# Seven products for a 2x2 block matrix product: another set, four of which are added up in PSUM

## The chip, the cores and the metric

One NeuronCore of a Trainium2 chip runs the whole program. The metric is the device time of one execution in microseconds (us). One execution was also recorded by the profiler; its span runs from the first to the last instruction. In the rows, PE is TensorE (PEld its weight loads), DVE is VectorE, ACT is ScalarE, POOL is GpSimd and SP is the engine that issues most transfers.

## The reference

Two layers over 512 tokens of width 1024. The part that changes is the second half of each layer's MLP:

```python
h = rms_norm(x, norm_ffn[l])
x = x + jnp.square(jax.nn.relu(h @ w_up[l])) @ w_down[l]      # w_up 1024x4096, w_down 4096x1024, float32
```

## The kernel before, in words

All matrix products run on float32 data that is split in two: a rounded high part (`whi`, `xhi`, `fhi`; written by ScalarE) and the rest (`wlo`, `xlo`, `flo`; written by VectorE, in some stages by GpSimd), and each product is three matmuls of 128x128 by 512 (low weights times high data, high by high, high weights by low data).

The MLP's 4096 hidden columns are worked in four quarters (`QUARTERS`) for each layer, eight in the program. A quarter has two phases:

- **Up.** Eight blocks of hidden columns (`up`, 24 matmuls of 512 columns each). ScalarE takes each block's relu and square into `hid` (`hidden`). After each pair j of blocks VectorE makes the factors from the 2x2 blocks A11, A12, A21, A22 (two halves of the tokens by two halves of the pair's columns), ScalarE writes their high parts (`factors_high`), VectorE their low ones (`factors_low`). A11's own parts are made ahead of the others (`a11_high`, `a11_low`).
- **Down.** The 2x2 block product with `w_down` is made from seven products instead of eight (a Strassen form). Product r takes one factor and one weight (a block of `w_down` or a sum of blocks), 24 matmuls: four pairs j, two token tiles k, three matmuls each, into two PSUM banks (k = 0 and 1). `PRODUCTS` names for each the factor, the pair of banks, and the blocks of `xt` (the residual) to which VectorE adds it (`add_product`): 12 blocks per quarter for each k, with 24 VectorE instructions.

Each product's weight is two rows of 128x1024 (g = 0, 1). They come by transfers into eight `raw` slots (four of them named `rawx`). Four of the products need sums of two blocks, made by transfers that GpSimd issues with an adding write (`add_block`); one sum is made by VectorE (`sum_m1`). ScalarE's copy to `whi` runs five rows (`SLOTS`) ahead of TensorE: it waits for `w_used`, which TensorE raises when a row's last matmul is done. `low` is the VectorE instruction behind it.

The order on each engine is written out by hand: TensorE's M3, M4, M2, M1, M6, M5, M7; VectorE's in the list at the end of the quarter's loop. A product that takes over a bank waits until VectorE has read the one before (`READ_BEFORE`: M1 after M3, M6 after M4, M5 after M2, M7 after M1), each time with two other products between. In a layer's last quarter the last two products run tile by tile (`last_products`), and the next norm, or in the second layer the final norm and the stores of the output, follows behind.

Of the kernel before, what the change touches and what calls it, by code (L numbers as in the profile page):

```python
# [37 lines left out]
A12, A11, A22, F1, F7, F2, F5, F6, A21 = range(9)  # L38
# [29 lines left out]
QUARTER_LOADS = (4, 4, 4, 4, 1, 1, 1, 1)  # L68
QUARTER_ADDS = 2
# [33 lines left out]
def block_loads(l, q, r, g):  # L103

    slot = PRODUCT_SLOT[r] + g
    late = 4 if r in (M6, M7) else 3 if r in (M3, M4) else 1
    return loads(l, slot) + MIX_LOADS[slot] + q * QUARTER_LOADS[slot] + late


def block_adds(l, q, r):  # L110

    return (l * QUARTERS + q) * QUARTER_ADDS + (2 if r in (M6, M7) else 1)
# [34 lines left out]
def summed_weights(l, q, g):  # L147

    return (l * QUARTERS + q) * 2 + g + 1
# [7 lines left out]
def adds_of(r):  # L157
    return len(PRODUCTS[r][2])


ADDS_DOWN = 2 * sum(adds_of(r) for r in range(len(PRODUCTS)))
# [9 lines left out]
def added_down(l, q, r, k):  # L171

    i = 2 * sum(adds_of(p) for p in range(r)) + (k + 1) * adds_of(r)
    if q == QUARTERS - 1 and r == M5:
        i += k * adds_of(M7)
    elif q == QUARTERS - 1 and r == M7:
        i -= (1 - k) * adds_of(M5)
    return l * ADDS + 2 * NT + q * ADDS_DOWN + i
# [20 lines left out]
def build(nc, x, gains, weights, sinks, ws, bs, alibi, ident_in, out):  # L199
    with ExitStack() as ctx:  # L200
# [31 lines left out]
        sb("rest", [P, 896])  # L232
# [90 lines left out]
        hid_ready = sem("hid_ready")  # L323
        factors_ready = sem("factors_ready")
# [41 lines left out]
        def _(sp):  # L366
# [3 lines left out]
            def load_mix(l, pos):  # L370
                if pos >= 4:
                    wait_low(sp, nth(l, pos - 4))
                elif l:
                    wait_low(sp, nth(l - 1, down_pos(QUARTERS - 1, M7 if pos < 2 else M6, pos % 2)))
                load(l * LAYER_ROWS + pos, mix_slot(pos))

            def load_up(l, q, i):
                if i >= 4:
                    wait_low(sp, nth(l, up_pos(q, i - 4)))
                elif q == 0:  # L380
                    wait_low(sp, nth(l, MLP_POS - 4 + i))
                else:
                    wait_low(sp, nth(l, down_pos(q - 1, M6 if i < 2 else M7, i % 2)))
                load(l * LAYER_ROWS + MLP_POS + q * QUARTER_ROWS + i, i % 4)

            def load_block(l, q, r, g):

                if r in (M3, M4):
                    wait_low(sp, nth(l, up_pos(q, 4 + PRODUCT_SLOT[r] + g)))
                elif r in (M6, M7):  # L390
                    wait_low(sp, nth(l, down_pos(q, M3 if r == M6 else M4, g)))
                elif q == 0:
                    sp.wait_ge(w_used, nth(l, wo_pos(1, 3)) + 1)
                else:
                    wait_low(sp, nth(l, down_pos(q - 1, M1 if r == M2 else M5, g)))
                load(block_row(l, q, PRODUCT_BLOCKS[r][0], g), PRODUCT_SLOT[r] + g)
# [25 lines left out]
            for l in range(DEPTH):  # L422
# [27 lines left out]
        def _(pool):  # L450
# [8 lines left out]
            def add_block(l, q, r, g):  # L459

                slot = PRODUCT_SLOT[r] + g
                pool.wait_ge(raw_landed[slot], 16 * block_loads(l, q, r, g))
                pool.dma_start(raw_at(slot), weights[block_row(l, q, PRODUCT_BLOCKS[r][1], g)], accum_op=ALU.add) \  # L463
                    .then_inc(sum_landed[slot], 16)

            for l in range(DEPTH):
                for pos in range(2 if l == 0 else 0, MLP_POS):
                    low(nth(l, pos))
                for q in range(QUARTERS):
                    for i in range(5 if q == 0 else 0):  # L470
                        low(nth(l, up_pos(q, i)))
                    for r in (M3, M4, M6, M7):
                        for g in range(2):
                            add_block(l, q, r, g)

        @block.tensor
        def _(pe):
            def three(o, hi, lo, n, wc, tokens, first, last, weights_move):

                s = n % SLOTS  # L480
                if weights_move:
                    pe.matmul(o, hi[:, tokens], wlo[:, s, wc], start=first, stop=False)  # L482
                    pe.matmul(o, hi[:, tokens], whi[:, s, wc], start=False, stop=False)  # L483
                    return pe.matmul(o, lo[:, tokens], whi[:, s, wc], start=False, stop=last)  # L484
                pe.matmul(o, wlo[:, s, wc], hi[:, tokens], start=first, stop=False)  # L485
                pe.matmul(o, whi[:, s, wc], hi[:, tokens], start=False, stop=False)  # L486
                return pe.matmul(o, whi[:, s, wc], lo[:, tokens], start=False, stop=last)  # L487
# [22 lines left out]
            def gate_values(l, s4, places):  # L510
# [3 lines left out]
                for i in places:  # L514
                    tokens = tok(order(2 * l)[i])
                    if s4 == 0:
                        pe.wait_ge(xlo_ready, 2 * l * 8 + i * 2 + 2)
                        if l:
                            pe.wait_ge(x_added, added_down(l - 1, QUARTERS - 1, M7 if i // 2 else M5, i % 2))
# [41 lines left out]
            def product_step(l, q, r, j, k):  # L561

                f = PRODUCTS[r][0]
                return three(bank(l, down_bank(q, r, k))[:, :], fhi[:, f - A11, j, :], flo[:, f - A11, j, :],
                             nth(l, down_pos(q, r, j // 2)), slice((j % 2) * 512, (j % 2 + 1) * 512), tok(k),
                             j == 0, j == PAIRS - 1, True)
# [8 lines left out]
            def product(l, q, r):  # L575

                for j in range(PAIRS):
                    if j % 2 == 0:
                        wait_low(pe, nth(l, down_pos(q, r, j // 2)))
                    if r in (M3, M4):  # L580
                        pe.wait_ge(hid_lo, ((l * QUARTERS + q) * PAIRS + j) * 2 + (2 if r == M4 else 1))
# [9 lines left out]
            def last_products(l, q, after):  # L591

                for k in range(2):
                    for r in (M5, M7):
# [9 lines left out]
                        after(2 * k + r - M5)  # L604
# [71 lines left out]
            def up(l, q, i, tokens=slice(0, SEQ)):  # L676
# [4 lines left out]
                elif i >= 2:  # L681
                    pe.wait_ge(x_added, added_down(l, q - 1, (M6, M5, M7)[i // 2 - 1], i % 2))
# [10 lines left out]
            for l in range(DEPTH):  # L693
# [71 lines left out]
                for q in range(QUARTERS):  # L765
                    for i in range(3 if q == 0 else 0, KC):
                        up(l, q, i).then_inc(w_used, 1)
                    for r in (M3, M4, M2, M1, M6):
                        product(l, q, r)
                    if q < QUARTERS - 1:  # L770
                        product(l, q, M5)
                        product(l, q, M7)
# [4 lines left out]
        def _(act):  # L777
            def high(n):
# [4 lines left out]
                else:  # L783
# [4 lines left out]
                    elif r in (M2, M5):  # L788
                        act.wait_ge(raw_landed[slot], 16 * block_loads(l, q, r, g))
                    elif r == M1:  # L790
                        act.wait_ge(weights_summed, summed_weights(l, q, g))
                    else:
                        act.wait_ge(sum_landed[slot], 16 * block_adds(l, q, r))
# [4 lines left out]
            def squares(norm, i):  # L798
# [6 lines left out]
                elif i < 2:  # L805
                    act.wait_ge(x_added, added_down(l - 1, QUARTERS - 1, M6, i))
                else:
                    act.wait_ge(x_added, added_down(l - 1, QUARTERS - 1, M7, i - 2))
# [32 lines left out]
            for l in range(DEPTH):  # L841
# [167 lines left out]
                def factors_high(q, j):  # L1009
                    act.wait_ge(factors_ready, (l * QUARTERS + q) * PAIRS + j + 1)  # L1010
                    act.copy(fhi[:, 1:, j, :], hid[:, A22:A21, :]).then_inc(hid_hi, 1)  # L1011

                for q in range(QUARTERS):
# [8 lines left out]
                    for n in range(down_pos(q, M3, 0), down_pos(q, M6, 1) if last else down_pos(q, M7, 1) + 1):  # L1022
# [10 lines left out]
            act.wait_ge(x_added, added_down(DEPTH - 1, QUARTERS - 1, M5, 1))  # L1033
            act.activation(z[:, 0, :], xt[:, last, 0:512], ACT.Square, accum_out=sspart[:, 0:1]).then_inc(part_summed, 1)
            act.wait_ge(x_added, added_down(DEPTH - 1, QUARTERS - 1, M7, 1))
# [11 lines left out]
        def _(dve):  # L1047
# [42 lines left out]
            for l in range(DEPTH):  # L1090
# [196 lines left out]
                def factors(q, j):  # L1287

                    dve.wait_ge(hid_ready, (l * QUARTERS + q) * KC + 2 * j + 2)
                    dve.tensor_tensor(hid[:, F1, :], hid[:, A11, :], hid[:, A22, :], ALU.subtract)  # L1290
                    outer = hid[:, A12:A21 + 1:A21 - A12, :]
                    dve.tensor_tensor(hid[:, F7:F2 + 1, :], outer, hid[:, A22:A22 + 1, :].broadcast_to([P, 2, HALF]),
                                      ALU.subtract)
                    dve.tensor_tensor(hid[:, F5:F6 + 1, :], outer, hid[:, A11:A11 + 1, :].broadcast_to([P, 2, HALF]),  # L1294
                                      ALU.subtract).then_inc(factors_ready, 1)

                def factors_low(q, j):
                    c = (l * QUARTERS + q) * PAIRS + j
                    dve.wait_ge(hid_hi, 2 * c + 2)
                    dve.tensor_tensor(flo[:, 1:, j, :], hid[:, A22:A21, :], fhi[:, 1:, j, :], ALU.subtract) \  # L1300
# [8 lines left out]
                def sum_m1(q, g):  # L1309

                    wait_low(dve, nth(l, down_pos(q, M2, g)))
                    dve.wait_ge(raw_landed[PRODUCT_SLOT[M5] + g], 16 * block_loads(l, q, M5, g))
                    b12, b21 = raw_at(PRODUCT_SLOT[M1] + g), raw_at(PRODUCT_SLOT[M5] + g)
                    dve.tensor_tensor(b12, b12, b21, ALU.subtract).then_inc(weights_summed, 1)

                def add_product(q, r, k):
# [5 lines left out]
                    for row, col, sign in PRODUCTS[r][2]:  # L1322
                        before = [(p, i) for p in range(r) for i, at in enumerate(PRODUCTS[p][2]) if at[:2] == (row, col)]
                        if before:
                            p, i = before[-1]
                            dve.wait_ge(x_added, added_down(l, q, p, k) - adds_of(p) + i + 1)
                        block = xt[:, 2 * row + k, col * 512:(col + 1) * 512]
                        dve.tensor_tensor(block, block, bank(l, down_bank(q, r, k))[:, :],  # L1328
                                          ALU.add if sign > 0 else ALU.subtract).then_inc(x_added, 1)
# [5 lines left out]
                for q in range(QUARTERS):  # L1335
# [8 lines left out]
                    low_down(q, M3, 0)  # L1344
                    factors_low(q, 1)
                    a11_low(q, 2)
                    low_down(q, M3, 1)
                    factors(q, 2)
                    low_down(q, M4, 0)
# [124 lines left out]
```

## Time and profile before

| | |
|---|---|
| time, median of 3 runs | 966.04 us (966.02 to 966.16) |
| time of the profiled execution | 966.15 us |
| its span | 964.1 us |
| TensorE busy | 952.1 us, 99% of the span |
| VectorE busy | 629.3 us, 65% |
| ScalarE busy | 487.0 us, 51% |
| GpSimd busy | 195.9 us, 20% |
| read from HBM | 146.87 MB, 155 GB/s over the span |

The profiled execution's own time is its span and 2.05 us that lie outside it. Busy shares are means over stages; matmuls overlap, so their listed length is longer than their spacing.

### The profile page before, as it was taken

The numbers are of one execution on the slowest core, as the hardware profiler recorded it, in microseconds if no ns is written. First come the engines' busy times: TensorE is split into PE (matmuls) and PEld (weight loads), VectorE is DVE, ScalarE is ACT, GpSimd is POOL, SyncE is SP. The second block draws the span as 40 slices with busy tenths as digits, with TensorE's granted clock in tenths as the row PEclk, the third lists the DMA queues.
The fourth block names the chain that finished last, engine by engine and source line by source line (L and its number), as shares of the span: only waits on it lengthen the run. The fifth ranks groups of instructions, "written<-read, shape, count | busy, mean of one in ns | idle before, by whom it ended". The sixth has DMA issues, their size and how long they took to land.

```text
span 964.1 us, 11765 instructions
## 1 busy us (share of the span) xinstructions
PE 952.1 (99%) x4624; PEld 789.8 (82%) x4624; DVE 629.3 (65%) x822; ACT 487.0 (51%) x735; POOL 195.9 (20%) x122
## 2 busy tenths in 40 slices
PE   8999999999999999999999999999999999999996
PEld 5888789888888888888888888898888888888885
DVE  5675523679459558756948752446966784695586
ACT  5566424653554464355455663355445535544553
POOL 2554215110110010011147434231001001100100
PEclk9999999999999999999999999999999999999998
DMA  9332114975883875687244322079377568838832
GB/s 294 139 110 88 52 58 144 244 158 158 250 185 92 263 185 118 212 219 153 88 137 139 102 67 79 32 234 243 91 265 184 119 186 234 182 99 247 193 82 88
DMA packets 42648, 149.74 MB, mean 155 GB/s; under 512 B 5857, under 2 KB 5985, under 8 KB 42593
## 3 DMA queue, kind: packets, MB, share of 16 engines
q1 hardware_dynamic: 33088, 114.84, 35.3%
q0 software_dynamic: 9216, 33.56, 19.9%
q8 instruction: 37, 0.61, 0.3%
q10 hardware_dynamic: 288, 0.59, 0.2%
q14 instruction: 19, 0.15, 0.1%
HBM read 146.87 MB, written 2.10 MB: 155 GB/s over the span
## 4 chain that ended last, share of the span: by engine, by line
PE 93%; DVE 3%; ACT 1%; DMA 1%; issue 1%; POOL 0%; SPq 0%; DVEq 0%
PE bank L485 16%; PE bank L487 16%; PE bank L486 16%; PE bank L482 14%; PE bank L484 14%; PE bank L483 14%; DVE xt L1328 1%; PE bank L507 1%; DVE wlo L1073 1%; PE bank L626 1%; DMA xt<-x_in 1%; PE bank L661 1%; PE bank L671 1%; PE bank L652 1%; ACT z L809 0%
## 5 line engine op out<-in xcount | busy, mean ns | idle before, releaser
L485 PE MATMUL bank<-xhi,wlo 128*128 128x512 f32 (+1 forms) x720 | 271.7, 377 | 0.0
L487 PE MATMUL bank<-xlo,whi 128*128 128x512 f32 (+1 forms) x720 | 270.1, 375 | 0.0
L486 PE MATMUL bank<-xhi,whi 128*128 128x512 f32 (+1 forms) x720 | 270.0, 375 | 0.0
L796 ACT ACTIVATE whi<-raw 128x1024 fp32r<-128x1024 f32 x172 | 181.3, 1056 | 131.8 <-PE bank L484 113.0
L456 POOL TENSOR_TENSOR wlo<-raw,whi 128x1024 fp32r<-128x1024 f32 x52 | 140.1, 2706 | 213.1 <-ACT whi L796 213.1
L482 PE MATMUL bank<-wlo,fhi 128*128 128x512 f32 x448 | 174.5, 389 | 0.0
L484 PE MATMUL bank<-whi,flo 128*128 128x512 f32 x448 | 174.3, 389 | 0.0
L483 PE MATMUL bank<-whi,fhi 128*128 128x512 f32 x448 | 174.3, 389 | 0.0
L1073 DVE TENSOR_TENSOR wlo<-raw,whi 128x1024 fp32r<-128x1024 f32 x120 | 145.6, 1226 | 25.8 <-ACT whi L796 25.8
L463 POOL DMA_DIRECT2D raw<-weights_in x64 | 55.4, 866 | 512.1 <-DMA raw<-weights_in 503.0
L487 PEld LDWEIGHTS bank<-xlo,whi 128*128 128x128 f32 x720 | 135.6, 188 | 24.6
L485 PEld LDWEIGHTS bank<-xhi,wlo 128*128 128x128 f32 x720 | 135.6, 188 | 24.5 <-issue 0.3
L486 PEld LDWEIGHTS bank<-xhi,whi 128*128 128x128 f32 x720 | 135.6, 188 | 23.8
L1328 DVE TENSOR_TENSOR xt<-xt,bank 128x512 f32<-128x512 f32 x192 | 120.1, 688 | 0.1
L997 ACT ACTIVATE z<-bank 128x512 f32<-128x512 f32 x64 | 38.3, 598 | 128.7 <-PE bank L487 128.7
L484 PEld LDWEIGHTS bank<-whi,flo 128*128 128x128 f32 x448 | 84.1, 188 | 17.6
L483 PEld LDWEIGHTS bank<-whi,fhi 128*128 128x128 f32 x448 | 84.1, 188 | 17.4
L482 PEld LDWEIGHTS bank<-wlo,fhi 128*128 128x128 f32 x448 | 84.1, 188 | 17.2
L796 ACT ACTIVATE whi<-rawx 128x1024 fp32r<-128x1024 f32 x48 | 50.8, 1058 | 52.2 <-PE bank L484 26.5
L1300 DVE TENSOR_TENSOR flo<-hid,fhi 128x1536 fp32r<-128x1536 f32 x32 | 56.3, 1758 | 13.2 <-ACT fhi L1011 13.2
L1290 DVE TENSOR_TENSOR hid<-hid 128x256 f32<-128x256 f32 x32 | 13.6, 425 | 73.7 <-ACT hid L1002 73.7
L1011 ACT CAST fhi<-hid 128x1536 fp32r<-128x1536 f32 x32 | 47.5, 1484 | 23.8 <-DVE hid L1294 23.8
(108 smaller groups left out, 957.4 us busy)
## 6 DMA issues: line engine op xcount, KB each, us to landing
raw<-weights_in SPq DMA_DIRECT2D x172, 512.0 KB, 4.1
raw<-weights_in POOLq DMA_DIRECT2D x64, 512.0 KB, 6.8
rawx<-weights_in SPq DMA_DIRECT2D x32, 512.0 KB, 6.8
xt<-x_in SPq DMA_DIRECT2D x4, 512.0 KB, 8.3
gbc<-gains_in SPq DMA_DIRECT2D x4, 512.0 KB, 5.1
out_t<-xt SPq DMA_DIRECT2D x3, 512.0 KB, 2.6
gbc<-gains_in ACTq DMA_DIRECT2D x1, 512.0 KB, 5.7
wst<-ws_in SPq DMA_DIRECT2D x2, 256.0 KB, 6.9
```

Of the source, the lines that this page charges most:

```text
L456: pool.tensor_tensor(wlo[:, n % SLOTS, :], raw_at(raw_slot(n)), whi[:, n % SLOTS, :], ALU.subtract) \
L463: pool.dma_start(raw_at(slot), weights[block_row(l, q, PRODUCT_BLOCKS[r][1], g)], accum_op=ALU.add) \
L482: pe.matmul(o, hi[:, tokens], wlo[:, s, wc], start=first, stop=False)
L483: pe.matmul(o, hi[:, tokens], whi[:, s, wc], start=False, stop=False)
L484: return pe.matmul(o, lo[:, tokens], whi[:, s, wc], start=False, stop=last)
L485: pe.matmul(o, wlo[:, s, wc], hi[:, tokens], start=first, stop=False)
L486: pe.matmul(o, whi[:, s, wc], hi[:, tokens], start=False, stop=False)
L487: return pe.matmul(o, whi[:, s, wc], lo[:, tokens], start=False, stop=last)
L796: act.activation(whi[:, n % SLOTS, :], raw_at(slot), ACT.Copy).then_inc(whi_ready, 1)
L1073: dve.tensor_tensor(wlo[:, n % SLOTS, :], raw_at(raw_slot(n)), whi[:, n % SLOTS, :], ALU.subtract) \
L1300: dve.tensor_tensor(flo[:, 1:, j, :], hid[:, A22:A21, :], fhi[:, 1:, j, :], ALU.subtract) \
L1328: dve.tensor_tensor(block, block, bank(l, down_bank(q, r, k))[:, :], ALU.add if sign > 0 else ALU.subtract).then_inc(x_added, 1)
```

## The change

The seven products are another set. Four of them (M6, M4, M5, M3) are no longer started on a cleared bank: they add onto the sum that already stands in the bank and that VectorE has just read (`ADDS_TO`: M6 onto M1, M4 onto M7, M5 onto M6, M3 onto M5). Each product then is added to one block of `xt`: 14 VectorE instructions per quarter in place of 24. TensorE's order is M1, M7, M6, M4, M5, M2, M3. The factors are made in three VectorE instructions as before, but the second needs the first and the third the second. GpSimd's adding transfers fall from eight rows per quarter to four (B12 onto B22 for M7, B12 onto B11 for M5), SP's loads of `w_down` from twelve to eight, and VectorE makes the weights of M6 and of M4 (four instructions of 128x1024 in place of two). The rest of the diff renames the products in the waits that other stages have on them (the next layer's, the norms').

```diff
-M3, M4, M2, M1, M6, M5, M7 = range(7)
-PRODUCTS = ((A11, 0, ((0, 0, 1), (1, 0, 1))), (A22, 1, ((0, 1, 1), (1, 1, 1))), (F2, 2, ((1, 1, 1), (1, 0, -1))),
-            (F1, 0, ((0, 1, 1), (1, 0, 1))), (F6, 1, ((1, 0, 1),)), (F5, 2, ((0, 0, 1), (0, 1, -1))),
-            (F7, 0, ((0, 1, 1),)))
-
-READ_BEFORE = {M1: M3, M6: M4, M5: M2, M7: M1}
+M1, M7, M6, M4, M5, M2, M3 = range(7)
+PRODUCTS = ((A11, 0, (0, 0, 1)), (S3, 1, (1, 1, -1)), (S2, 0, (1, 0, 1)), (A22, 1, (1, 0, 1)), (S5, 0, (1, 1, -1)),
+            (A12, 2, (0, 0, 1)), (S4, 0, (0, 1, -1)))
+
+ADDS_TO = {M6: M1, M4: M7, M5: M6, M3: M5}
...
-PRODUCT_SLOT = (0, 2, 4, 4, 0, 6, 2)
-PRODUCT_BLOCKS = ((B11, B21), (B22, B12), (B12,), None, (B11, B12), (B21,), (B22, B21))
+PRODUCT_SLOT = (0, 2, 6, 6, 0, 4, 2)
+PRODUCT_BLOCKS = (B11, B22, None, None, None, B21, B22)
...
+                elif r == M3:
+                    wait_low(sp, nth(l, down_pos(q, M7, g)))
+                    sp.wait_ge(weights_summed, summed_weights(l, q, M6, g))
...
-                    for r in (M2, M5, M3, M4, M6, M7):
+                    for r in (M2, M1, M7, M3):
...
+            def add_b12(l, q, r, g):
 
                 slot = PRODUCT_SLOT[r] + g
+                if r == M7:
+                    pool.wait_ge(raw_landed[slot], 16 * block_loads(l, q, M7, g))
+                else:
+                    wait_low(pool, nth(l, down_pos(q, M1, g)))
+                    pool.wait_ge(weights_summed, summed_weights(l, q, M6, g))
+                pool.dma_start(raw_at(slot), weights[block_row(l, q, B12, g)], accum_op=ALU.add) \
...
-                             j == 0, j == PAIRS - 1, True)
+                             j == 0 and r not in ADDS_TO, j == PAIRS - 1, True, r in ADDS_TO)
...
-                if r in READ_BEFORE:
-                    pe.wait_ge(x_added, added_down(l, q, READ_BEFORE[r], k))
+                if r in ADDS_TO:
+                    pe.wait_ge(x_added, added_down(l, q, ADDS_TO[r], k))
...
-                    for r in (M5, M7):
+                    for r in (M2, M3):
...
-                    for r in (M3, M4, M2, M1, M6):
+                    for r in (M1, M7, M6, M4, M5):
...
                     dve.wait_ge(hid_ready, (l * QUARTERS + q) * KC + 2 * j + 2)
-                    dve.tensor_tensor(hid[:, F1, :], hid[:, A11, :], hid[:, A22, :], ALU.subtract)
-                    outer = hid[:, A12:A21 + 1:A21 - A12, :]
-                    dve.tensor_tensor(hid[:, F7:F2 + 1, :], outer, hid[:, A22:A22 + 1, :].broadcast_to([P, 2, HALF]),
-                                      ALU.subtract)
-                    dve.tensor_tensor(hid[:, F5:F6 + 1, :], outer, hid[:, A11:A11 + 1, :].broadcast_to([P, 2, HALF]),
-                                      ALU.subtract).then_inc(factors_ready, 1)
+                    made = ((l * QUARTERS + q) * PAIRS + j) * 2
+                    dve.tensor_tensor(hid[:, S3:S5 + 1, :], hid[:, A11:A22 + 1:A22 - A11, :],
+                                      hid[:, A21:A21 + 1, :].broadcast_to([P, 2, HALF]), ALU.subtract).then_inc(factor_made, 1)
+                    dve.wait_ge(factor_made, made + 1)
+                    dve.scalar_tensor_tensor(hid[:, S2, :], hid[:, S5, :], -1.0, hid[:, A11, :], ALU.mult, ALU.subtract) \
+                        .then_inc(factor_made, 1)
+                    dve.wait_ge(factor_made, made + 2)
+                    dve.scalar_tensor_tensor(hid[:, S4, :], hid[:, S2, :], -1.0, hid[:, A12, :], ALU.mult, ALU.subtract) \
+                        .then_inc(factors_ready, 1)
...
+                def sum_m6(q, g):
+
+                    dve.wait_ge(sum_landed[PRODUCT_SLOT[M7] + g], 16 * block_adds(l, q))
+                    dve.wait_ge(raw_landed[PRODUCT_SLOT[M1] + g], 16 * block_loads(l, q, M1, g))
...
+                    dve.tensor_tensor(raw_at(PRODUCT_SLOT[M6] + g), raw_at(PRODUCT_SLOT[M7] + g),
+                                      raw_at(PRODUCT_SLOT[M1] + g), ALU.add).then_inc(weights_summed, 1)
+
+                def sum_m4(q, g):
+
+                    wait_low(dve, nth(l, down_pos(q, M6, g)))
+                    dve.wait_ge(raw_landed[PRODUCT_SLOT[M2] + g], 16 * block_loads(l, q, M2, g))
+                    t2 = raw_at(PRODUCT_SLOT[M4] + g)
+                    dve.tensor_tensor(t2, t2, raw_at(PRODUCT_SLOT[M2] + g), ALU.add).then_inc(weights_summed, 1)
...
                     a11_low(q, 3)
+                    sum_m6(q, 0)
+                    low_down(q, M7, 1)
+                    factors(q, 3)
+                    sum_m6(q, 1)
+                    low_down(q, M6, 0)
+                    factors_low(q, 3)
+                    sum_m4(q, 0)
+                    low_down(q, M6, 1)
+                    sum_m4(q, 1)
+                    add_both(q, M1)
+                    low_down(q, M4, 0)
                     low_down(q, M4, 1)
-                    factors(q, 3)
-                    low_down(q, M2, 0)
-                    factors_low(q, 3)
-                    low_down(q, M2, 1)
-                    sum_m1(q, 0)
-                    sum_m1(q, 1)
-                    add_both(q, M3)
-                    low_down(q, M1, 0)
-                    low_down(q, M1, 1)
-                    add_both(q, M4)
-                    low_down(q, M6, 0)
-                    low_down(q, M6, 1)
-                    add_both(q, M2)
+                    add_both(q, M7)
                     low_down(q, M5, 0)
                     low_down(q, M5, 1)
-                    add_both(q, M1)
-                    low_down(q, M7, 0)
-                    low_down(q, M7, 1)
+                    add_both(q, M6)
+                    low_down(q, M2, 0)
+                    low_down(q, M2, 1)
+                    add_both(q, M4)
+                    low_down(q, M3, 0)
+                    low_down(q, M3, 1)
```

## Rows read from the trace of the kernel before

**Rows 1.** The page: span and busy time of the engines
```profile
span 964.1 us, 11765 instructions
...
PE 952.1 (99%) x4624; PEld 789.8 (82%) x4624; DVE 629.3 (65%) x822; ACT 487.0 (51%) x735; POOL 195.9 (20%) x122
```

**Rows 2.** Windows by stage (stretch, length, busy us and count by engine, PE clock, DMA share, GB/s)
```profile
649.00:731.00 82.00, 82.00 (x364) 67.91 (x363) 59.14 (x70) 41.23 (x49) 6.90 (x8) 1.00 0.73 199
...
894.00:964.00 70.00, 61.04 (x270) 50.22 (x268) 49.72 (x64) 32.43 (x45) 5.20 (x6) 0.96 0.46 116
```

**Rows 3.** Timeline, TensorE, third product of two quarters (start us, length us, engine, line)
```profile
682.65 0.39 PE L484 MATMUL bank<-whi,flo 128*128 128x512 f32 x1
682.88 0.39 PE L482 MATMUL bank<-wlo,fhi 128*128 128x512 f32 x1
...
764.48 0.39 PE L482 MATMUL bank<-wlo,fhi 128*128 128x512 f32 x1
```

**Rows 4.** Timeline, TensorE, first layer, a restart after a wait
```profile
21.05 0.50 PE L482 MATMUL bank<-wlo,xhi 128*128 128x512 f32 x1 [0.40 <-POOL wlo L456]
21.39 0.39 PE L483 MATMUL bank<-whi,xhi 128*128 128x512 f32 x1
```

**Rows 5.** Timeline, VectorE, from the last factors of a quarter on
```profile
673.49 0.42 DVE L1290 TENSOR_TENSOR hid<-hid 128x256 f32<-128x256 f32 x1 [2.56 <-ACT hid L1002]
673.83 0.68 DVE L1292 TENSOR_TENSOR hid<-hid 128x512 f32<-128x512 f32 x1
674.43 0.68 DVE L1294 TENSOR_TENSOR hid<-hid 128x512 f32<-128x512 f32 x1
675.04 1.22 DVE L1073 TENSOR_TENSOR wlo<-rawx,whi 128x1024 fp32r<-128x1024 f32 x1
676.67 1.76 DVE L1300 TENSOR_TENSOR flo<-hid,fhi 128x1536 fp32r<-128x1536 f32 x1 [0.41 <-ACT fhi L1011]
678.34 1.22 DVE L1073 TENSOR_TENSOR wlo<-rawx,whi 128x1024 fp32r<-128x1024 f32 x1
679.48 2.35 DVE L1314 TENSOR_TENSOR rawx<-rawx 128x1024 f32<-128x1024 f32 x2
681.75 2.47 DVE L1328 TENSOR_TENSOR xt<-xt,bank 128x512 f32<-128x512 f32 x4
```

**Rows 6.** Timeline, ScalarE, the same stretch
```profile
675.15 1.48 ACT L1011 CAST fhi<-hid 128x1536 fp32r<-128x1536 f32 x1 [0.74 <-DVE hid L1294]
...
683.13 1.06 ACT L796 ACTIVATE whi<-raw 128x1024 fp32r<-128x1024 f32 x1 [0.21 <-PE bank L484]
```

**Rows 7.** Timeline, VectorE, an operation that needs the one before it
```profile
63.09 1.22 DVE L1156 TENSOR_REDUCE rowmax<-band 128x8 f32<-128x1024 f32 x1
64.34 0.23 DVE L1159 TENSOR_SCALAR negmax<-rowmax,sink 128x8 f32<-128x8 f32 x1
```

**Rows 8.** Instructions by line, VectorE (line, operation, count, busy us, mean ns, idle before)
```profile
L1105 DVE SCALAR_TENSOR_TENSOR pp<-pp,bank 128x512 f32<-128x512 f32 x16 | 10.9, 684 | 22.5 <-ACT pp L857 22.5
...
L1121 DVE SCALAR_TENSOR_TENSOR gv<-gsum,gv 128x512 f32<-128x512 f32 x8 | 7.1, 882 | 0.3
```

**Rows 9.** The page: GpSimd's transfers, KB each, median us to landing
```profile
raw<-weights_in POOLq DMA_DIRECT2D x64, 512.0 KB, 6.8
```

**Rows 10.** Timeline, VectorE, the end of the kernel
```profile
945.18 1.30 DVE L1328 TENSOR_TENSOR xt<-xt,bank 128x512 f32<-128x512 f32 x2
...
950.36 2.07 DVE L1328 TENSOR_TENSOR xt<-xt,bank 128x512 f32<-128x512 f32 x3
...
955.44 1.28 DVE L1328 TENSOR_TENSOR xt<-xt,bank 128x512 f32<-128x512 f32 x2
...
958.18 0.68 DVE L1328 TENSOR_TENSOR xt<-xt,bank 128x512 f32<-128x512 f32 x1
```

**Rows 11.** Timeline, TensorE, the last quarter's last stretch
```profile
944.00 0.39 PE L482 MATMUL bank<-wlo,fhi 128*128 128x512 f32 x1
...
954.65 0.39 PE L484 MATMUL bank<-whi,flo 128*128 128x512 f32 x1
```

More of the change, by code:

```diff
@@ L144, in block_row, with summed_weights @@
     return l * LAYER_ROWS + MLP_POS + q * QUARTER_ROWS + KC + 2 * b + g
-def summed_weights(l, q, g):
-    return (l * QUARTERS + q) * 2 + g + 1
+def summed_weights(l, q, r, g):
+    return (l * QUARTERS + q) * 4 + (2 if r == M4 else 0) + g + 1
 def order(norm):
     return (2, 3, 0, 1) if norm and norm % 2 == 0 else (0, 1, 2, 3)
-def adds_of(r):
-    return len(PRODUCTS[r][2])
-ADDS_DOWN = 2 * sum(adds_of(r) for r in range(len(PRODUCTS)))
+ADDS_DOWN = 2 * len(PRODUCTS)
 ADDS = 2 * NT + QUARTERS * ADDS_DOWN
@@ L171, in added_down @@
 def added_down(l, q, r, k):
[L173 to L177, printed above, removed]
+    i = 2 * r + k + 1
+    if q == QUARTERS - 1 and r == M2:
+        i += k
+    elif q == QUARTERS - 1 and r == M3:
+        i -= 1 - k
     return l * ADDS + 2 * NT + q * ADDS_DOWN + i
@@ L471, in _, with three @@
                         low(nth(l, up_pos(q, i)))
-                    for r in (M3, M4, M6, M7):
+                    for r in (M7, M5):
                         for g in range(2):
-                            add_block(l, q, r, g)
+                            add_b12(l, q, r, g)
         @block.tensor
         def _(pe):
-            def three(o, hi, lo, n, wc, tokens, first, last, weights_move):
+            def three(o, hi, lo, n, wc, tokens, first, last, weights_move, on_sum=False):
                 s = n % SLOTS
                 if weights_move:
[L482 to L487, printed above, removed]
+                    pe.matmul(o, hi[:, tokens], wlo[:, s, wc], start=first, stop=False, skip_group_check=on_sum)
+                    pe.matmul(o, hi[:, tokens], whi[:, s, wc], start=False, stop=False, skip_group_check=on_sum)
+                    return pe.matmul(o, lo[:, tokens], whi[:, s, wc], start=False, stop=last, skip_group_check=on_sum)
+                pe.matmul(o, wlo[:, s, wc], hi[:, tokens], start=first, stop=False, skip_group_check=on_sum)
+                pe.matmul(o, whi[:, s, wc], hi[:, tokens], start=False, stop=False, skip_group_check=on_sum)
+                return pe.matmul(o, whi[:, s, wc], lo[:, tokens], start=False, stop=last, skip_group_check=on_sum)
             def columns(o, n, hi, lo, tokens=slice(0, SEQ), before_chunk=None):
@@ L603, in last_products @@
                                 mm.then_inc(w_used, 1)
-                        after(2 * k + r - M5)
+                        after(2 * k + r - M2)
             def project(l, pos, before_chunk=None):
@@ L1021, in _ @@
                     last = q == QUARTERS - 1
-                    for n in range(down_pos(q, M3, 0), down_pos(q, M6, 1) if last else down_pos(q, M7, 1) + 1):
+                    for n in range(down_pos(q, M1, 0), down_pos(q, M5, 1) if last else down_pos(q, M3, 1) + 1):
                         hi(n + SLOTS)
@@ L1321, in add_product @@
                         dve.wait_ge(w_used, nth(l, down_pos(q, r, 1)) + 1)
[L1322 to L1329, printed above, removed]
+                    row, col, sign = PRODUCTS[r][2]
+                    before = [p for p in range(r) if PRODUCTS[p][2][:2] == (row, col)]
+                    if before:
+                        dve.wait_ge(x_added, added_down(l, q, before[-1], k))
+                    block = xt[:, 2 * row + k, col * 512:(col + 1) * 512]
+                    dve.tensor_tensor(block, block, bank(l, down_bank(q, r, k))[:, :],
+                                      ALU.add if sign > 0 else ALU.subtract).then_inc(x_added, 1)
                 def add_both(q, r):
@@ L1404, in _ @@
             scaled(1)
-            add_product(last, M5, 0)
-            add_product(last, M7, 0)
+            add_product(last, M2, 0)
+            add_product(last, M3, 0)
             scaled(2)
-            add_product(last, M5, 1)
+            add_product(last, M2, 1)
             dve.wait_ge(part_summed, 1)
@@ L1412, in _ @@
             dve.tensor_tensor(xt[:, t, 0:512], xt[:, t, 0:512], gbc[:, 0:512], ALU.mult).then_inc(gained, 1)
-            add_product(last, M7, 1)
+            add_product(last, M3, 1)
             close(norm, NT - 1)
```

94 lines of the change are left out of this document (43 added, 51 removed).

## The prediction

> **What bounds the kernel now.** The page first: TensorE is busy for 952.1 of 964.1 us, VectorE for 629.3 [rows 1]. The windows by stage then say whether this is so inside a quarter: from 649 to 731 us TensorE is busy for 82.00 of 82.00 us, at a granted clock of 1.00; only the last window, which holds the end, has 9 us without it [rows 2]. The timeline gives the pace. The third product's first matmul starts at 682.88 in one quarter and at 764.48 in the next [rows 3]: 81.60 us for 15 products and blocks of 24 matmuls, 360 in all, so 226.7 ns each and 5.44 us for a product. There is no slack in TensorE's queue and no wait either. Both sets have seven products of 24 matmuls, so the change can gain nothing inside a quarter. It can lose there, where TensorE has to wait for VectorE, and it can gain at the end of the kernel, where VectorE runs behind TensorE. So I ask two questions: does VectorE now come in time, and how much shorter is the tail.
>
> **The new wait, step by step.** M6 is third and adds onto M1's bank. It may start when VectorE has read M1, with only M7 between. Before, the tightest such wait had two products between (10.88 us), now 5.44 us. The wait stands ahead of M6's first weight load. TensorE's own time for M6's first matmul is 682.88 in the quarter of the rows [rows 3]. VectorE's first add of M1 stands behind a list of work that begins when the last factors can be made, at 673.49, when ScalarE's square of the quarter's last block has come [rows 5]. That start hangs on TensorE's last up block, so it keeps its distance to M6 in every quarter. The list:
>
> - Factors. Now three independent instructions; VectorE starts the next 0.34 us after one of 256 columns and 0.60 us after one of 512 (673.49, 673.83, 674.43, 675.04) [rows 5]. In the new chain each needs the result before it. A row of such a pair: 63.09 + 1.22 = 64.31, the next at 64.34, so 0.03 us behind the end [rows 7]. A scalar_tensor_tensor of 512 columns takes 684 ns like a tensor_tensor [rows 8], so I give the 256-column one the 0.42 us of its neighbour [rows 5]. 0.68 + 0.03 + 0.42 + 0.03 = 1.16, and 0.34 to the next start: 675.00, as before within 0.04. Three instructions replace three.
> - sum_m6(1): 1.14 us (679.48 to 681.75 is two of them [rows 5]): to 676.14. Low part of M6's first row, 1.14 (678.34 to 679.48): 677.28. Factors' low parts, 1.67 (676.67 to 678.34): 678.95. ScalarE's high parts are done at 676.63 [rows 6], so the 0.41 us that VectorE waits for them before is gone.
> - sum_m4(0), 1.14: 680.09. Low part of M6's second row, and sum_m4(1) behind it needs it finished: 1.22 + 0.03: 681.34. sum_m4(1), 1.14: 682.48. First add of M1: 0.68, done 683.16.
>
> Before, the add of the first product starts at 681.75 [rows 5], and nobody waits. Now it starts 0.73 us later and its reader comes 5.44 us earlier. Release to weight load 0.05 us (an estimate, from the 0.04 to 0.05 us that engines take to start after a release in these timelines): 683.21. After such a wait the next matmul starts 0.34 us behind the first (21.05 to 21.39 [rows 4]) and not 0.23, since the first has its weight load in front: 0.11 more. So M6 runs from 683.32 in place of 682.88: **0.45 us lost in a quarter, 3.6 us in eight**. Tile k = 1 needs the second add, 0.60 later (683.81), and its weight load is due at 682.65 + 0.68 + 0.45 = 683.78: nothing more.
>
> On this chain the Trainium skill (VectorE: DVE Perf Modes, "The DRAIN you can't avoid") states another price: the pipeline empties after every VectorE instruction anyway and a semaphore after each costs nothing extra. By that the three places where one instruction needs the one before cost nothing and M1's add comes 0.35 us earlier. The trace disagrees: without a wait the next instruction starts 0.08 us before the end of the one ahead, with it 0.03 us after [rows 5, 7]. I go by the rows and keep that case as a rival.
>
> **The other waits in a quarter.** M4 waits for M7 (read at 686.0 to 687.2, needed at 688.7), M5 for M6 (690.1, needed 694.2), M3 for M5 (700, needed 705): VectorE then has two low parts (2.3 us) and two adds (1.2 us) for 5.44 us of TensorE, where before it had 2.3 and mostly 2.4. They catch up. ScalarE's copies for M4 wait for sum_m4 (done 680.2 and 682.6) and for nothing on TensorE; they are done by 683.7. All hidden.
>
> **Transfers.** Eight fewer plain and adding rows of 512 KB in a quarter; nothing waits for the old ones on TensorE, so their loss is worth 0. New is that B12 onto B11 for M5 can only be issued after sum_m6, at about 676.3 for the second row. GpSimd's take 6.8 us to land [rows 9]: 684, against ScalarE's copy of it at about 686. If it came late, VectorE's adds of M6 would move, and these have 4 us of slack. SP's load of M3's row, behind the same wait, is needed at about 695; the next quarter's loads stand behind it in SP's queue, but wait for low parts of M5 that come later. Cost 0, bounded by 0 and by one more such stall if a landing took over 14 us.
>
> **The tail.** In the last quarter TensorE's last two products run tile by tile from 944.00 and its last matmul starts at 954.65 [rows 11], so its banks are readable at 955.13 (a ScalarE copy starts 0.48 us after the start of the matmul that it waits for, 682.65 to 683.13 [rows 3, 6]). But VectorE makes the last add only at 958.18 [rows 10]: it is 3.05 us behind, with two blocks for each tile of old M5 and with a backlog from the adds before. That is the most that can be had. New, with the quarter's stall in it (TensorE at 944.45 where it was at 944.00):
>
> - M5's first row is free on TensorE at 939.01 + 2.49 + 0.48 = 941.98; ScalarE's copy of the last row 1.05, VectorE's low part from 943.1, then add of M5 at 944.28, where the same step (old M6) was at 945.18.
> - From there to the adds of the next product 5.18 us (945.18 to 950.36, two norms of ScalarE and VectorE [rows 10]): 949.46. Before, three adds, the third from 951.74 as it needs the second on the same block (950.36 + 2.07 - 0.69). Now M2 at 949.46, M3 as its bank comes, at 947.17 + 2.49 + 0.48 = 950.14.
> - From that add's start to the next tile 3.70 (951.74 to 955.44): 953.85; one add in place of two, then to the last add 2.14 from its start (second of the two at 956.04, to 958.18): 955.99. TensorE's bank is ready at 955.58.
>
> So the last add starts at 955.99 in place of 958.18: 2.19 us earlier with this quarter's stall, **2.64 us without it**. Bounds: 1.2 (only the doubled adds fall away) and 3.05. The turn between the layers has no wait of TensorE before and its adds come earlier too: 0.
>
> **Sum.** 3.6 - 2.64 = +0.96 us: a span of 965.1 from 964.1, and with 2.05 us outside it 967.1 against 966.15; on the median of 966.04, 967.0 us. What this kernel can tell from no change is 0.2%, 1.9 us: no change.
>
> **Rivals.**
>
> - *VectorE comes in time.* If chained instructions cost nothing, M1's add is done 0.35 us earlier, the stall is 0.10 us in a quarter, and 0.8 - 2.64 gives 964.2; without any stall 963.4. For it: the stall is a difference of 0.5 us between two sums of nine terms. Against: rows 7, and each term is a row of this kernel. The skill's sentence on waits that cost nothing, cited above, speaks for the same case. Faster only below 0.09 us of stall.
> - *The factor chain or the sums are longer*, the slower case. No row shows a scalar_tensor_tensor of two SBUF inputs in 256 columns behind its source. The nearest chained one, gv, has a mean of 882 ns for 512 columns against 684 for the others [rows 8], 0.2 more. At 0.15 more for each of two the stall is 0.75 us: 6.0 - 2.64, 969.4. Against: gv runs beside GpSimd's low parts and reads a broadcast, and neither is so here. It decides from a stall of 0.57 us.
> - *The tail gives only 1.2 us.* Then 3.6 - 1.2: 968.4, just slower. For it: the chain of norms sets the distance of the adds, not the number of adds.
> - *The stalls drop TensorE's clock.* Against: it waited 0.40 us at 21.05 and the next matmul followed the first in 0.34 us [rows 4], and the granted clock stands at 1.00, the level of 2.4 GHz, in the saturated stages [rows 2]. 1 in 50.
>
> **Chances.** My case 0.64; in time 0.10; longer chain or clock 0.19; short tail 0.07. Its own range, from stalls of 0.36 to 0.55 and tails of 2.4 to 3.0: 965.9 to 968.0, a little of it past the bound. Faster 0.10, same 0.65, slower 0.25. For 8 in 10: from 964.6, leaving out the case without a stall, to 969.4, leaving out the worse of the longer chains.
>
> **What would show it.** Eight idle places of TensorE at the third product, each about 0.4 us, with VectorE's xt as their releaser, and none at the other six; a quarter of 82.05 us and not 81.60; matmuls at 226.7 ns elsewhere; VectorE's first add of M1 at 9.0 us behind the start of the last factors; last add 1.3 us behind the start of the last matmul or less; GpSimd and SP later than nobody. The prediction is wrong if TensorE also waits at M4, M5 or M3, if the first add comes over 9.1 us or under 8.7 us behind the factors, or if the adding transfers for M5 hold ScalarE.

## The result, and the profile after

Over 22 executions each, the changed kernel takes 967.48 us (967.36 to 967.74) and the one before 966.06 (965.88 to 966.53). The ratio is 1.0015, with a 95% interval of 1.0009 to 1.0020: 1.4 us more. That is within the 0.2% that the prediction called no change, but it is a real loss: the fastest of the changed executions is slower than the slowest of the others.

The page of the changed kernel:

```profile
span 965.8 us, 11653 instructions
...
PE 954.9 (99%) x4624; PEld 789.6 (82%) x4624; DVE 599.3 (62%) x758; ACT 486.2 (50%) x735; POOL 168.6 (17%) x90
...
PEclk9999999999999999999999999999999999999999
...
HBM read 113.32 MB, written 2.10 MB: 119 GB/s over the span
...
raw<-weights_in POOLq DMA_DIRECT2D x32, 512.0 KB, 5.9
```

TensorE's busy time is 2.8 us longer than in [rows 1] with the same count of matmuls: the ends of matmuls are modelled, and about half of each new wait is listed as busy (of the 0.54 us by which a quarter is longer, 0.28 are idle in the windows below). That is 2.1 of the 2.8 us; 0.5 more are at the start, before the first quarter. VectorE has 30 us less to do and 33.6 MB less comes from memory, and neither makes a quarter shorter.

The waits of TensorE's matmuls in this execution (who waited for whom, us in total, times, longest):

```profile
PE bank L486 <- DVE xt L1343: 2.2, 8, 0.3
PE bank L691 <- DVE pp L1080: 2.0, 1, 2.0
PE bank L486 <- POOL wlo L455: 0.4, 1, 0.4
```

The last two lines are of the start and stand before too. The first is new: eight waits for VectorE's adds, one for each quarter. The windows from one quarter's last factors to the next (two of the six that can be laid so; the others lie within 0.03 us of them) give the length of a quarter:

```profile
284.79:366.93 82.14, 81.86 (x362) 67.51 (x361) 53.76 (x61) 39.71 (x47) 3.45 (x4) 1.00 0.46 129
...
757.91:840.06 82.15, 81.88 (x362) 67.51 (x361) 53.76 (x60) 39.70 (x47) 3.45 (x4) 1.00 0.46 129
```

82.14 us in place of the 81.60 of [rows 3]: 0.54 us. Read at the matmuls before and behind each of the eight waits, the losses are 0.53 to 0.56 us, 4.35 us together. The granted clock is 1.00 in all six windows.

VectorE's timeline from the last factors to M1's adds, which answers to [rows 5]:

```profile
675.78 0.69 DVE L1295 TENSOR_TENSOR hid<-hid 128x512 f32<-128x512 f32 x1 [2.07 <-ACT hid L1006]
676.51 0.42 DVE L1298 SCALAR_TENSOR_TENSOR hid<-hid 128x256 f32<-128x256 f32 x1
676.97 0.42 DVE L1301 SCALAR_TENSOR_TENSOR hid<-hid 128x256 f32<-128x256 f32 x1
677.31 1.22 DVE L1322 TENSOR_TENSOR rawx<-raw 128x1024 f32<-128x1024 f32 x1
678.45 1.22 DVE L1077 TENSOR_TENSOR wlo<-rawx,whi 128x1024 fp32r<-128x1024 f32 x1
679.58 1.75 DVE L1307 TENSOR_TENSOR flo<-hid,fhi 128x1536 fp32r<-128x1536 f32 x1
681.25 1.22 DVE L1330 TENSOR_TENSOR rawx<-rawx 128x1024 f32<-128x1024 f32 x1
682.38 1.22 DVE L1077 TENSOR_TENSOR wlo<-rawx,whi 128x1024 fp32r<-128x1024 f32 x1
683.63 1.22 DVE L1330 TENSOR_TENSOR rawx<-rawx 128x1024 f32<-128x1024 f32 x1
684.78 1.28 DVE L1343 TENSOR_TENSOR xt<-xt,bank 128x512 f32<-128x512 f32 x2
```

L1322 is sum_m6(1), L1330 sum_m4. Each chained instruction starts 0.03 to 0.04 us after the end of the one before (675.78 + 0.69 to 676.51; 682.38 + 1.22 to 683.63), each other one 0.08 us before it. M1's first add starts 684.78 - 675.78 = 9.00 us after the factors. What TensorE and its weight loads make of it, in two views:

```profile
684.94 0.39 PE L488 MATMUL bank<-whi,flo 128*128 128x512 f32 x1
685.60 0.47 PE L486 MATMUL bank<-wlo,fhi 128*128 128x512 f32 x1 [0.28 <-DVE xt L1343]
685.91 0.40 PE L487 MATMUL bank<-whi,fhi 128*128 128x512 f32 x1
686.14 0.39 PE L488 MATMUL bank<-whi,flo 128*128 128x512 f32 x1
```

```profile
685.57 0.19 PEld L486 LDWEIGHTS bank<-wlo,fhi 128*128 128x128 f32 x1 [0.67 <-issue]
```

L486 is M6's first matmul. Without a wait it would have come at 684.94 + 0.23 = 685.17. The add ends at 685.46; the weight load starts at 685.57; the second matmul, at 685.91, would have come at 685.40. So 0.51 us are lost there, and the first matmuls after it follow each other in 0.23 us and not 0.227, which makes the rest of 0.54.

The end of the kernel on VectorE, which answers to [rows 10], and TensorE's last matmul, to [rows 11]:

```profile
948.23 1.28 DVE L1343 TENSOR_TENSOR xt<-xt,bank 128x512 f32<-128x512 f32 x2
...
953.41 1.38 DVE L1343 TENSOR_TENSOR xt<-xt,bank 128x512 f32<-128x512 f32 x2
...
957.80 0.68 DVE L1343 TENSOR_TENSOR xt<-xt,bank 128x512 f32<-128x512 f32 x1
...
959.94 0.68 DVE L1343 TENSOR_TENSOR xt<-xt,bank 128x512 f32<-128x512 f32 x1
```

```profile
959.11 0.39 PE L488 MATMUL bank<-whi,flo 128*128 128x512 f32 x1
```

The last add starts 0.83 us after the start of the last matmul. Before it was 958.18 - 954.65 = 3.53. The tail is 2.70 us shorter, measured from TensorE. The last matmul itself starts 4.46 us later (959.11 against 954.65): the 4.35 us of the eight waits and 0.1 in which one execution differs from another (in the first experiment below, which has no such wait, it starts at 954.88). 4.46 - 2.70 = 1.76 us, and the spans differ by 1.7.

### The profile page after: what moved, and what is told of

Its sections match the earlier page's. It is cut to its first block, busy times and chain, and to the rows that moved or that the text cites. A ratio compares the mean times of both kernels' runs of the same rounds, so it can differ in the third digit from the quotient of the medians.

```text
span 965.8 us, 11653 instructions
## 1 busy us (share of the span) xinstructions
PE 954.9 (99%) x4624; PEld 789.6 (82%) x4624; DVE 599.3 (62%) x758; ACT 486.2 (50%) x735; POOL 168.6 (17%) x90
## 4 chain that ended last, share of the span: by engine, by line
PE 88%; DVE 7%; issue 3%; ACT 2%; POOL 0%; DVEq 0%; ACTq 0%
PE bank L489 16%; PE bank L491 16%; PE bank L490 16%; PE bank L486 12%; PE bank L488 11%; PE bank L487 11%; DVE rawx L1330 2%; DVE wlo L1077 1%; PE bank L511 1%; DVE rawx L1322 1%; DVE xt L1343 1%; PE bank L691 1%; PE bank L630 1%; PE bank L665 1%; PE bank L675 1%
## 5 line engine op out<-in xcount | busy, mean ns | idle before, releaser
L486 PE MATMUL bank<-wlo,fhi 128*128 128x512 f32 x448 | 175.2, 391 | 2.2 <-DVE xt L1343 2.2
L466 POOL DMA_DIRECT2D raw<-weights_in x32 | 27.8, 868 | 545.3 <-DMA raw<-weights_in 385.6
L486 PEld LDWEIGHTS bank<-wlo,fhi 128*128 128x128 f32 x448 | 84.1, 188 | 22.5 <-issue 5.3
L1343 DVE TENSOR_TENSOR xt<-xt,bank 128x512 f32<-128x512 f32 x112 | 71.8, 679 | 0.0
L1295 DVE TENSOR_TENSOR hid<-hid 128x512 f32<-128x512 f32 x32 | 22.2, 692 | 70.1 <-ACT hid L1006 70.0
L1077 DVE TENSOR_TENSOR wlo<-rawx,whi 128x1024 fp32r<-128x1024 f32 x48 | 57.8, 1218 | 8.8 <-ACT whi L800 8.8
```

The lines of the kernel that those rows point to most:

```text
L1077: dve.tensor_tensor(wlo[:, n % SLOTS, :], raw_at(raw_slot(n)), whi[:, n % SLOTS, :], ALU.subtract) \
```

## The experiments

Times are medians. The kernel before was measured again beside them: 966.19 us beside the order, the chain and the two runs on the tail, 966.08 us beside the longer list, the cleared banks and the transfers, 966.09 us beside the last version.

### Is it VectorE's order?

```diff
-                    sum_m4(q, 1)
                     add_both(q, M1)
+                    sum_m4(q, 1)
```

> The changed kernel with M1's two adds ahead of sum_m4(1) in VectorE's order. If the cost is only VectorE's list before the first add: the add starts 1.2 us earlier, 7.8 us behind the start of the last factors in place of 9.0, TensorE has no wait at M6, a quarter takes 81.60 us and not 82.14, the tail's 2.7 us stay: 963.4 us. Rival, adding onto a read bank or the chained factors cost TensorE time by themselves: the quarter stays above 81.8 us and the time above 965.

963.25 us, ratio 0.9970 (0.9959 to 0.9981) to the kernel before, as are all ratios below. Its VectorE timeline and a window from one quarter's last factors to the next:

```profile
673.73 0.69 DVE L1295 TENSOR_TENSOR hid<-hid 128x512 f32<-128x512 f32 x1 [2.07 <-ACT hid L1006]
...
679.19 1.22 DVE L1330 TENSOR_TENSOR rawx<-rawx 128x1024 f32<-128x1024 f32 x1
680.33 1.22 DVE L1077 TENSOR_TENSOR wlo<-rawx,whi 128x1024 fp32r<-128x1024 f32 x1
681.46 1.28 DVE L1343 TENSOR_TENSOR xt<-xt,bank 128x512 f32<-128x512 f32 x2
682.66 1.22 DVE L1330 TENSOR_TENSOR rawx<-rawx 128x1024 f32<-128x1024 f32 x1
```

```profile
284.37:365.96 81.59, 81.59 (x362) 67.56 (x361) 53.78 (x60) 39.70 (x47) 3.45 (x4) 1.00 0.46 129
```

The add starts 7.73 us after the factors and ends at 682.14. By the distances of [rows 3, 5] M6's first weight load is due 9.16 us after the factors, at 682.89, so VectorE is 0.75 us early; the quarter is 81.59 us, and TensorE's list of waits has only the two of the start. The instructions are the same and so are the chained factors and the four products that add onto a sum: the whole loss in the quarters was one VectorE instruction in the wrong place. The rival, that these cost TensorE time themselves, falls.

### What does a chained instruction cost?

```diff
-                    dve.wait_ge(factor_made, made + 1)
-                    dve.scalar_tensor_tensor(hid[:, S2, :], hid[:, S5, :], -1.0, hid[:, A11, :], ALU.mult, ALU.subtract) \
+                    dve.scalar_tensor_tensor(hid[:, S2, :], hid[:, A22, :], -1.0, hid[:, A11, :], ALU.mult, ALU.subtract) \
                         .then_inc(factor_made, 1)
-                    dve.wait_ge(factor_made, made + 2)
-                    dve.scalar_tensor_tensor(hid[:, S4, :], hid[:, S2, :], -1.0, hid[:, A12, :], ALU.mult, ALU.subtract) \
+                    dve.scalar_tensor_tensor(hid[:, S4, :], hid[:, A22, :], -1.0, hid[:, A12, :], ALU.mult, ALU.subtract) \
```

> The changed kernel with the second and third factor made from A22 in place of the result before them, so without the two waits (the values of S2 and S4 are others). If a chained VectorE instruction costs the 0.12 us that the rows show: two of them 0.24 us in a quarter, stall 0.30 in place of 0.54, 1.9 us in all: 965.5 us. Rival, by the Trainium skill's section on the DRAIN, a semaphore between two VectorE instructions costs nothing: 967.5 us.

965.62 us, 1.86 below the changed kernel's 967.48; each against the kernel before measured beside it (-0.57 and +1.42), 1.99. VectorE's factors, and the window of a quarter:

```profile
284.27 0.69 DVE L1294 TENSOR_TENSOR hid<-hid 128x512 f32<-128x512 f32 x1 [2.30 <-ACT hid L1006]
284.88 0.42 DVE L1296 SCALAR_TENSOR_TENSOR hid<-hid 128x256 f32<-128x256 f32 x1
285.21 0.42 DVE L1298 SCALAR_TENSOR_TENSOR hid<-hid 128x256 f32<-128x256 f32 x1
285.55 1.22 DVE L1319 TENSOR_TENSOR rawx<-raw 128x1024 f32<-128x1024 f32 x1
```

```profile
284.27:366.16 81.89, 81.86 (x362) 67.49 (x361) 53.07 (x60) 39.70 (x47) 3.45 (x4) 1.00 0.46 129
```

The list is 1.28 us from the first factor to the next other work (284.27 to 285.55) and not 1.53 (675.78 to 677.31), and the quarter is 81.89 us, 0.25 less. So a wait of a VectorE instruction on the one in front of it costs 0.12 us here, and that 0.25 reaches the end eight times. The Trainium skill (VectorE: DVE Perf Modes, "The DRAIN you can't avoid") says that a semaphore behind each instruction costs nothing extra, from a measurement of eight copies; with the float32 instructions of this list the measurement is against it, and decides.

M6's restart in the same quarter:

```profile
293.02 1.28 DVE L1340 TENSOR_TENSOR xt<-xt,bank 128x512 f32<-128x512 f32 x2
293.43 0.39 PE L488 MATMUL bank<-whi,flo 128*128 128x512 f32 x1
293.81 0.19 PEld L486 LDWEIGHTS bank<-wlo,fhi 128*128 128x128 f32 x1 [0.42 <-issue]
```

The first add ends at 293.02 + 0.68 = 293.70, and M6's first matmul would have come at 293.43 + 0.23 = 293.66. An add that is 0.04 us late by this reckoning costs 0.29 us; the last section comes back to it.

### One more us on the list

```diff
                     sum_m4(q, 1)
+                    low_down(q, M4, 0)
                     add_both(q, M1)
-                    low_down(q, M4, 0)
```

> The changed kernel with the low part of M4's first row also ahead of M1's adds: one more VectorE instruction of 1.14 us on the list. If each us on the list is a us of TensorE's wait: stall 1.68 us in a quarter in place of 0.54, 9.1 us in all: 976.6 us, granted clock still 1.00 inside the quarters. Rival, the clock falls at waits over 1 us: more than 985.

976.50 us, ratio 1.0108 (1.0093 to 1.0123). One of TensorE's waits, and a window of a quarter:

```profile
213.48 0.47 PE L486 MATMUL bank<-wlo,fhi 128*128 128x512 f32 x1 [1.41 <-DVE xt L1343]
```

```profile
285.82:369.08 83.26, 81.85 (x362) 67.49 (x361) 53.95 (x61) 39.70 (x47) 3.46 (x4) 1.00 0.45 127
```

The quarter is 83.26 us: 1.12 more than 82.14 for one instruction of 1.14 us. From the list without sum_m4(1) (no loss) over the one without the chain (0.29) and the changed one (0.54) to this (1.66) what is added to VectorE's list once TensorE waits for it is added to the quarter, eight times. Against the kernels before measured beside them the changed kernel stands at +1.42 us and this one at +10.42: 9.0 more, for eight times 1.12. TensorE's idle 1.41 us leaves the granted clock at 1.00.

### Does adding onto a sum cost TensorE anything?

```diff
-                             j == 0 and r not in ADDS_TO, j == PAIRS - 1, True, r in ADDS_TO)
+                             j == 0, j == PAIRS - 1, True)
```

> The changed kernel with every product started on a cleared bank (M6, M4, M5 and M3 then lack the sum that they should add onto), all waits as they were. If adding onto a sum is free for TensorE: 967.5 us, quarter 82.14 us. Rival, it costs time at the start of each of the four products: less, down to 963.4.

967.42 us, against 967.48 with the sums. The quarter is 82.12 us and TensorE has the same eight waits for VectorE's adds, 2.2 us in all. Adding onto the sum costs nothing that these runs can tell.

### Do the transfers matter?

```diff
-QUARTER_ADDS = 2
+QUARTER_ADDS = 1
...
-                    for r in (M3, M4, M6, M7):
+                    for r in (M3, M4):
...
-                    elif r in (M2, M5):
+                    elif r in (M2, M5, M6, M7):
```

> The kernel before without the adding transfers for its M6 and M7 (their weights are then one block each): four fewer adding rows in a quarter. If transfers are hidden: 966.1 us. Rival, they slow the engines' access to the buffers: some tenths of a us to 2 us less.

966.15 us against 966.08, ratio 1.000 (0.9991 to 1.001). GpSimd's transfers fall from 64 to 32 and 16.8 MB less are read, and it is worth nothing. Fewer plain loads were not tried, so for them this is argued: no wait of TensorE in a quarter of the kernel before names a transfer.

### Where does the tail's gain come from?

First one product of the kernel before, then all, with fewer adds:

```diff
-            (F1, 0, ((0, 1, 1), (1, 0, 1))), (F6, 1, ((1, 0, 1),)), (F5, 2, ((0, 0, 1), (0, 1, -1))),
+            (F1, 0, ((0, 1, 1), (1, 0, 1))), (F6, 1, ((1, 0, 1),)), (F5, 2, ((0, 0, 1),)),
```

> The kernel before with old M5 added to one block of xt in place of two (the other sum is left out). If doubled adds in the tail make it late: last add 1.4 us earlier, 964.7 us. Rival, the norms' chain alone sets the tail: 966.0 us.

```diff
-PRODUCTS = ((A11, 0, ((0, 0, 1), (1, 0, 1))), (A22, 1, ((0, 1, 1), (1, 1, 1))), (F2, 2, ((1, 1, 1), (1, 0, -1))),
-            (F1, 0, ((0, 1, 1), (1, 0, 1))), (F6, 1, ((1, 0, 1),)), (F5, 2, ((0, 0, 1), (0, 1, -1))),
+PRODUCTS = ((A11, 0, ((0, 0, 1),)), (A22, 1, ((1, 1, 1),)), (F2, 2, ((1, 1, 1),)),
+            (F1, 0, ((0, 1, 1),)), (F6, 1, ((1, 0, 1),)), (F5, 2, ((0, 0, 1),)),
```

> The kernel before with each of its seven products added to one block of xt (the other sums are left out): 14 adds in a quarter as in the changed kernel, with the old waits, which had slack. If the tail's gain is all from the adds, half from the doubled ones of the last products and half from VectorE's backlog before: 963.4 us. Rival, the backlog has no part: 964.7, as with M5 alone. Rival, the gain needs the other set of products: 966.

964.44 and 963.64 us against 966.19: 1.75 and 2.55 us, ratios 0.9982 (0.9973 to 0.9991) and 0.9973 (0.9963 to 0.9984). VectorE's tail in the first:

```profile
945.11 1.28 DVE L1328 TENSOR_TENSOR xt<-xt,bank 128x512 f32<-128x512 f32 x2
...
950.27 1.28 DVE L1328 TENSOR_TENSOR xt<-xt,bank 128x512 f32<-128x512 f32 x2
...
954.56 0.68 DVE L1328 TENSOR_TENSOR xt<-xt,bank 128x512 f32<-128x512 f32 x1
...
956.70 0.68 DVE L1328 TENSOR_TENSOR xt<-xt,bank 128x512 f32<-128x512 f32 x1
```

```profile
954.56 0.39 PE L484 MATMUL bank<-whi,flo 128*128 128x512 f32 x1
```

and in the second (each with the last matmul behind it):

```profile
943.86 1.28 DVE L1328 TENSOR_TENSOR xt<-xt,bank 128x512 f32<-128x512 f32 x2
...
949.01 1.39 DVE L1328 TENSOR_TENSOR xt<-xt,bank 128x512 f32<-128x512 f32 x2
...
953.77 0.68 DVE L1328 TENSOR_TENSOR xt<-xt,bank 128x512 f32<-128x512 f32 x1
...
955.91 0.68 DVE L1328 TENSOR_TENSOR xt<-xt,bank 128x512 f32<-128x512 f32 x1
```

```profile
954.74 0.39 PE L484 MATMUL bank<-whi,flo 128*128 128x512 f32 x1
```

TensorE's last matmul starts at 954.56 in the first run and at 954.74 in the second, so measured from there the last add has come 1.39 us nearer in the first (2.14 in place of 3.53) and 2.36 us in the second (1.17). In the first the adds of old M6 start as in [rows 10], at 945.11: this part is the doubled adds of the last products, as expected. In the second they start at 943.86: the backlog is gone and the wait for ScalarE's copy sets the start, as in the changed kernel. Measured from TensorE these adds come 1.43 us nearer (1.25 and the 0.18 by which TensorE is later), but only 0.97 of it reaches the last add, where 1.3 was expected. The rest is lost between the adds at 949.01 and the next tile's scaling: 3.56 us, against 3.09 in the first run and 3.19 in the changed kernel (953.41 to 956.60). There 0.46 us of idle time stand ahead of the scaling, behind a reciprocal that it needs; why is left open. Neither run has the other set of products: 2.36 of the 2.70 us of the tail come from the count of adds alone, and the set as such is not needed for them. In both runs the medians fall by 0.27 us more than the last add (958.18 to 956.70 and to 955.91); 0.14 and 0.18 of it lie outside the span.

### A version that beats both

To the order of the first experiment one exchange in the tail is added:

```diff
-            scaled(2)
             add_product(last, M2, 1)
+            scaled(2)
```

> The kernel with M1's adds first, and in the tail M2's add of the last tile ahead of the scaling of the tile before it. With M1's adds first alone the last add starts 0.35 us after its bank can be read (955.71 against 954.88 + 0.48). If only VectorE's order holds it: the last add comes as its bank does, 0.35 us earlier, 962.9 us. Rival, the norm of that tile is what counts and now comes later: 963.2 us or more.

962.72 us, ratio 0.9966 (0.9952 to 0.9980), against 0.9970 (0.9959 to 0.9981) for the first experiment: the intervals overlap, and what the exchange does is read from the trace. VectorE's two adds of the last tile:

```profile
952.42 0.69 DVE L1343 TENSOR_TENSOR xt<-xt,bank 128x512 f32<-128x512 f32 x1 [2.03 <-PE bank L488]
...
955.15 0.68 DVE L1343 TENSOR_TENSOR xt<-xt,bank 128x512 f32<-128x512 f32 x1
```

The last add starts at 955.15 with the last matmul at 954.72, 0.43 us behind it, where it was 0.83 us behind in the first experiment (955.71 against 954.88). The add at 952.42, which does wait for its bank, starts 0.42 us behind the start of the matmul that it waits for (952.00). So the last add comes as its bank does, and can't come earlier. Of the 0.56 us by which it is earlier than in the first experiment, 0.40 is the exchange; by the other 0.16 the last matmul itself is earlier, as executions differ.

## Why the prediction was right

- **What bounds it.** TensorE has no slack in a quarter and the change gives it no work less: right, and the run in which VectorE comes in time has a quarter of 81.59 us.
- **VectorE's list.** Forecast 8.99 us (673.49 to 682.48) from factors to the first add, measured 9.00. Each term held: the chain 1.51 against 1.53, the sums and low parts 1.14, the factors' low parts 1.67.
- **The stall.** Forecast 0.45 us, measured 0.54. The place and the cause held: M1's add done 0.28 us after M6's first matmul was due, measured 0.29. The term that was mis-sized is the time from release to weight load, which I had as an estimate of 0.05 us: it is 0.11 (685.46 to 685.57). The rest of the restart is 0.11 us as forecast, and 0.03 more is lost in the next matmuls. Eight times 0.09 is 0.7 us, and the span of 965.8 us lies that far above the forecast 965.1; the median of 967.48 lies 0.5 above 967.0, as 1.8 us lie outside the span in the profiled execution (967.63 - 965.8) and not 2.05. "No change" was close: by the prediction's own rule a stall of 0.57 us is slower, and it was 0.54.
- **The tail.** Forecast 2.64, measured 2.70. With TensorE's times taken off, each step lies within 0.1 us of its forecast. Of its two causes the doubled adds are worth 1.39 us at the last add (the prediction's lower bound put them at 1.2); the backlog alone showed 1.0 us, where the experiment expected 1.3.
- **The other waits.** None at M4, M5 and M3, as forecast. The transfers cost nothing, as forecast, but one sign that I had named as counting against the prediction did come, in one quarter of eight: ScalarE's copy of M5's second row waited for GpSimd's adding transfer in the first quarter.

```profile
215.55 1.06 ACT L800 ACTIVATE whi<-raw 128x1024 fp32r<-128x1024 f32 x1 [1.80 <-DMA raw<-weights_in]
```

  That transfer took 9.6 us to land (issue at 205.92). TensorE did not wait, since VectorE's adds of M6 have the slack that the prediction counted (no wait is listed ahead of M5). So the part "GpSimd later than nobody" was wrong, and the stated condition was too wide: it should have been a wait that reaches TensorE.
- **Rivals.** VectorE in time: not so, the two chained factors cost 0.25 us and the third chained place, sum_m4(1), another 0.12, about the 0.35 that the rows gave; even with two of the three waits out, 0.29 us were lost. A longer chain: no, 0.42 us for each scalar_tensor_tensor. A short tail of 1.2: no. A lower clock: no, the windows stand at 1.00 with waits of up to 1.41 us.

## What to carry to other kernels

When the bounding engine has no wait at all, taking work from another engine gains only where that engine is behind, here the tail. What is left is to look for the place where the distance between a result and its reader gets shorter, and to add up the helper's list up to it, instruction by instruction. The loss here came from the order and not from the amount of work: with 30 us less of VectorE's work the kernel was slower, until one instruction of 1.14 us changed places with the two adds for which TensorE waits. Put what the bounding engine waits for as early in the helper's order as its inputs allow.

## What was not expected of the hardware

VectorE's deadline here was not M6's first matmul but its weight load, 0.23 us earlier. In a stream without a wait the weight load starts together with the matmul ahead of it (682.89 and 682.88 in the first experiment). Against that time each of the three runs with a wait loses what VectorE is late, to 0.02 us:

| | weight load due | first add ends | late | lost in the quarter |
|---|---|---|---|---|
| without the chain | 293.43 | 293.70 | 0.27 us | 0.29 us |
| the changed kernel | 684.94 | 685.46 | 0.52 us | 0.54 us |
| one more instruction | 211.68 | 213.34 | 1.66 us | 1.66 us |

Against the matmul's own time (685.17 in the changed kernel) the same three adds are late by 0.04, 0.29 and 1.43 us, and 0.23 to 0.25 us more are lost than that. In the changed kernel these are 0.11 us from the end of the add to the weight load (the same 0.11 in all three runs), 0.11 until the matmuls stand in their old distance (0.34 us from one to the next at such a restart in [rows 4], less the usual 0.23), and 0.03 in the matmuls behind. The first experiment's add ends 0.75 us ahead of the weight load and loses nothing; no run lies between the two.
